# The bias of 30 experts copied into PSUM by ScalarE instead of multiplied in by TensorE

## The reference, cut to what matters

```python
def moe_ffn(h, w_router, b_router, w_gate_up, b_gate_up, w_down, b_down):
    logits = (xt @ w_router + b_router).astype(jnp.float32)
    top_val, top_idx = lax.top_k(logits, TOP_K)          # 4 of 32
    gates = jax.nn.softmax(top_val, axis=-1)
    ...
    def expert_block(args):                              # 128 tokens of one expert
        xb, e = args
        gu = xb @ w_gate_up[e] + b_gate_up[e]            # (128,1024) x (1024,2048)
        gate = jnp.minimum(gu[:, :D_FF], SWIGLU_LIMIT)
        up = jnp.clip(gu[:, D_FF:], -SWIGLU_LIMIT, SWIGLU_LIMIT)
        glu = gate * jax.nn.sigmoid(SWIGLU_ALPHA * gate)
        return ((up + 1.0) * glu) @ w_down[e] + b_down[e]
    ys = ys * slot_g[:, None]                            # each row by its gate
    out = jax.ops.segment_sum(ys, slot_tok, num_segments=T)
```

## Time and profile before

| | |
|---|---|
| time before, median of 3 (range) | 1756.38 us (1755.71 to 1757.04) |
| profiled execution: its time, its span | 1755.91 us, 1754.3 us |
| TensorE busy | 1731.1 us (99%) |
| VectorE busy | 1339.7 us (76%); 940.07 of the 1000 us from 700 to 1700 |
| ScalarE busy | 1120.1 us (64%) |
| GpSimd busy | 293.3 us (17%) |
| HBM traffic | 476.22 MB read, 28.36 MB written |

### The profile page before, as it was taken

One profiled execution on the slowest core, in us unless ns is written; L12 is line 12 of the kernel. 1 busy time (PEld: TensorE's weight loads), 2 busy tenths in 40 slices (PEclk: granted clock), 3 DMA queues, 4 the chain that ended last, 5 costly groups with the idle time before them and its releaser, 6 DMA issues.

```text
span 1754.3 us, 23536 instructions
## 1 busy us (share of the span) xinstructions
PE 1731.1 (99%) x8315; PEld 1410.9 (80%) x8316; DVE 1339.7 (76%) x1169; ACT 1120.1 (64%) x957; POOL 293.3 (17%) x228
## 2 busy tenths in 40 slices
PE   9999999999999999999999999999999999999996
PEld 7777888888887777888888888888888888888885
DVE  6323324343346898999999999999999999999998
ACT  5534334473222467777777777777777777777777
POOL 3000000000001262222222121212121212121211
PEclk9999999999999999999999999999999999999998
DMA  8322231212332599999999999999999999999995
GB/s 293 95 96 72 75 93 51 70 57 88 101 139 85 214 348 397 357 384 385 402 367 372 368 385 373 369 377 384 370 373 380 385 369 367 381 388 369 371 367 210
DMA packets 115728, 487.96 MB, mean 278 GB/s; under 512 B 18931, under 2 KB 49683, under 8 KB 66528
## 3 DMA queue, kind: packets, MB, share of 16 engines
q1 hardware_dynamic: 99576, 455.76, 67.9%
q0 software_dynamic: 16096, 31.54, 6.4%
q10 hardware_dynamic: 8, 0.01, 0.0%
HBM read 476.22 MB, written 28.36 MB: 288 GB/s over the span
## 4 chain that ended last, share of the span: by engine, by line
PE 94%; DVE 3%; ACT 2%; issue 1%; POOLq 0%; POOL 0%; DVEq 0%; ACTq 0%
PE psA L1717 22%; PE psA L1718 22%; PE psA L1719 22%; PE psX L1719 6%; PE psX L1718 6%; PE psX L1717 6%; PE psX L1724 3%; DVE wlo L1464 1%; PE psX L1911 1%; PE psX L1896 1%; PE psA L2128 1%; ACT whi L1003 1%; PE psX L1920 1%; PE psA L2008 0%; PE psX L1856 0%
## 5 line engine op out<-in xcount | busy, mean ns | idle before, releaser
L1464 DVE TENSOR_TENSOR wlo<-raw,whi 128x2048 fp32r<-128x2048 f32 x382 | 863.6, 2289 | 61.2 <-ACT whi L1003 60.2
L1003 ACT CAST whi<-raw 128x2048 fp32r<-128x2048 f32 x382 | 724.8, 1913 | 197.3 <-PE psA L1719 178.5
L1717 PE MATMUL psA<-whi,xT_hi 128*128 128x512 f32 x1036 | 408.3, 394 | 1.9 <-issue 1.9
L1719 PE MATMUL psA<-whi,xT_lo 128*128 128x512 f32 x1036 | 404.0, 390 | 0.0
L1718 PE MATMUL psA<-wlo,xT_hi 128*128 128x512 f32 x1036 | 403.9, 390 | 0.0
L1717 PEld LDWEIGHTS psA<-whi,xT_hi 128*128 128x128 f32 x1036 | 195.0, 188 | 43.1 <-issue 3.9
L1719 PEld LDWEIGHTS psA<-whi,xT_lo 128*128 128x128 f32 x1036 | 194.8, 188 | 40.7
L1718 PEld LDWEIGHTS psA<-wlo,xT_hi 128*128 128x128 f32 x1036 | 195.1, 188 | 39.6 <-issue 0.5
L1717 PE MATMUL psX<-whi,aT_hi 128*128 128x512 f32 x496 | 195.8, 395 | 0.0
L1719 PE MATMUL psX<-whi,aT_lo 128*128 128x512 f32 x496 | 193.5, 390 | 0.0
L1718 PE MATMUL psX<-wlo,aT_hi 128*128 128x512 f32 x496 | 193.3, 390 | 0.0
(11 more groups left out here) (408 smaller groups left out, 2025.2 us busy)
## 6 DMA issues: line engine op xcount, KB each, us to landing
raw<-in_w_gate_up SPq DMA_DIRECT2D x254, 1024.0 KB, 8.7
raw<-in_w_down SPq DMA_DIRECT2D x128, 1024.0 KB, 8.1
raw<-in_w_in SPq DMA_DIRECT2D x32, 1024.0 KB, 5.5
raw<-in_w_gla_proj SPq DMA_DIRECT2D x4, 1024.0 KB, 5.1
raw<-in_w_fox_proj SPq DMA_DIRECT2D x4, 1024.0 KB, 5.3
raw<-in_w_out SPq DMA_DIRECT2D x4, 1024.0 KB, 5.0
xt<-in_x SPq DMA_DIRECT2D x4, 512.0 KB, 7.3
h_dram<-xt POOLq DMA_DIRECT2D x4, 512.0 KB, 6.0
```

What stands on the lines that cost most here:

```text
L1003: s_.copy(xsplit(c)[0], xraw(slot)).then_inc(hi_ready, 1)
L1464: v.tensor_tensor(lo, xraw(slot), hi.bitcast(F32), ALU.subtract).then_inc(lo_ready, 1)
L1717: mm(dst, sh, mh, start=first, stop=False)
L1719: return mm(dst, sl, mh, start=False, stop=last)
```

## The change

From expert 2 on the bias no longer goes through TensorE.

- GpSimd loads the bias row of expert e (four pieces of 512 floats on partitions 0, 32, 64, 96) into `bias_row` and copies each over all 128 partitions with `partition_broadcast` into `bias_all` (128x4x512). The spread for expert i+2 stands in body i behind the gather and ahead of the scatter.
- ScalarE copies `bias_all` into `psA` (`seed(i+1)`, after expert i's silu) once VectorE has read the banks (`up_ev`) and the broadcasts are done (`bias_spread`); TensorE's first matmul of the next `gate_up` waits for `seeded`, and all of its matmuls add to what is there.
- `gate_up_bias` is gone for experts 2 to 31. Experts 0 and 1 and overflow blocks keep it.
- VectorE clips before its last subtraction of the body, waiting for the last gate-up tile (`tile_used`), and makes `act_t` before the first subtraction of the next expert. Its three copies are gone.
- GpSimd copies `gidx` and `didx` itself; ScalarE takes the gate column straight from `ltab`.
- Several one-shot semaphores are merged, and `lnffn_g` lies at another address.

```diff
+        def gather_index(i):
+            pool.wait_ge(index_ready, 2 * i - 3)
+            pool.wait_ge(xg_in, 16 * (i + 1))
+            g.tensor_copy(gidx[:], lrows[:, bass.ds(i + 2, 1)]).then_inc(index_ready, 1)
+        def scatter_index(i):
+            pool.wait_ge(y_out, 16 * (i - 1))
+            g.tensor_copy(didx[:], lrows[:, bass.ds(i - 1, 1)]).then_inc(index_ready, 1)
...
+        def load_row(e):
+            pool.wait_ge(bias_spread, 4 * (e - 2))
+            g.dma_start(bias_row[0:P:32, :], a["b_gate_up"][0][e].rearrange("(n c) -> n c", c=512)).then_inc(brow_in, 16)
+        def spread_row(e):
+            pool.wait_ge(brow_in, 16 * (e - 1))
+            pool.wait_ge(xg_in, 16 * e)
+            if isinstance(e, int) and e == 2:
+                pool.wait_ge(gu_done, 2)
+            else:
+                if not isinstance(e, int) or e > 3:
+                    pool.wait_ge(y_out, 16 * (e - 3))
+                pool.wait_ge(seeded, e - 2)
+            for n in range(4):
+                g.partition_broadcast(bias_all[:, n, :], bias_row[32 * n:32 * n + 1, :]).then_inc(bias_spread, 1)
+            pool.wait_ge(bias_spread, 4 * (e - 1))
...
         pool.wait_ge(routed, 1)
-        pool.wait_ge(gu_done, 2)
+        g.dma_start(bias_row[0:P:32, :], a["b_gate_up"][0][2].rearrange("(n c) -> n c", c=512)).then_inc(brow_in, 16)
+        spread_row(2)
         g.dma_start(lnffn_g[:], bcast(a["ln_ffn_g"][0])).then_inc(lnffn_in, 16)
...
         def body(i, last):
             if not last:
-                pool.wait_ge(gu_done, i + 1)
-                load_bgu(i + 1)
                 if not isinstance(i, int) or i < E - 2:
-                    gather(i + 3, i + 2)
+                    load_row(i + 2)
+                    if isinstance(i, int) and i == 1:
+                        gather(4, 3)
+                    else:
+                        gather_index(i)
+                        gather(None, i + 2)
             if isinstance(i, int) and 3 <= i < 3 + TT:
                 add_bias(i - 3, i)
+            if not last and (not isinstance(i, int) or i < E - 2):
+                spread_row(i + 2)
+            if not last and (not isinstance(i, int) or 2 <= i < E - 2):
+                scatter_index(i)
             scatter(i - 1)
...
+        def seed(e):
+            act.wait_ge(up_ev, e)
+            act.wait_ge(bias_spread, 4 * (e - 1))
+            s_.copy(psA[:], bias_all[:]).then_inc(seeded, 1)
...
             silu(i)
+            seed(i + 1)
             for c in range(XSPL):
                 step_hi(i + 1, c)
-            y_evac(i - 1, i + 3)
+            y_evac(i - 1)
...
-            if not first:
-                dve.wait_ge(y_out, 16 * (i - 1))
-                chain.mark(v.tensor_copy(didx[:], lrows[:, bass.ds(i - 1, 1)]))
-                chain.mark(v.tensor_copy(queue[:, 0, 1:2], ltab[:, bass.ds(i - 1, 1), 1]))
-                dve.wait_ge(xg_in, 16 * (i + 1))
-                chain.join()
-                v.tensor_copy(gidx[:], lrows[:, bass.ds(i + 2, 1)]).then_inc(tab_ready, 1)
...
-            for c in range(XSPL + 5, STEPC):
+            for c in range(XSPL + 5, STEPC - 1):
                 step_lo(i, c)
             swiglu_in(i)
+            step_lo(i, STEPC - 1)
             turned_lo(xT_hi_s, i + 2, xT_hi, xT_lo, xT_lo_s)
-            step_lo(i + 1, 0)
             swiglu_out(i)
-            for c in range(1, XSPL):
+            for c in range(XSPL):
                 step_lo(i + 1, c)
...
+        def gate_up_seeded(n, c):
+            tile_ready(n)
+            hi, lo = xsplit(c)
+            for b in range(4):
+                cols = slice(b * 512, (b + 1) * 512)
+                mm(psA[:, b, :], xT_hi[:, c, :], hi[:, cols], start=False, stop=False, skip_group_check=True)
...
-                pe.wait_ge(up_ev, i)
+                pe.wait_ge(seeded, i - 1)
...
-            gate_up_bias(i)
+            if first:
+                gate_up_bias(i)
```

More of the change, by code:

```diff
@@ L205, in build @@
     tokens = at("tokens", 104.5, [P, P])
-    lnffn_g = at("lnffn_g", 120, [P, D])
+    lnffn_g = at("lnffn_g", 203, [P, D])
     lnffn_b = at("lnffn_b", 172, [P, D])
@@ L756, in _ @@
                 e = pool.value_load(ovtab[0:1, bass.ds(j, 1)], min_val=0, max_val=E - 1)
-                gather(E + 4 + j, E + j)
+                gather(6 + j, E + j)
                 load_bgu(e)
@@ L1065, in y_evac_over, with y_evac @@
                           scale=queue[:, 0, 1:2]).then_inc(y_ready, 1)
-        def y_evac(i, free, src=psD):
+        def y_evac(i):
             act.wait_ge(tile_used, down_used(i))
-            act.wait_ge(tab_ready, free)
-            s_.activation(y_t[:], src.rearrange("p b c -> p (b c)"), ACT.Copy,
-                          scale=queue[:, 0, 1:2]).then_inc(y_ready, 1)
+            if isinstance(i, int) and i == 0:
+                act.wait_ge(tab_ready, 4)
+                gate = queue[:, 0, 1:2]
+            else:
+                act.wait_ge(y_out, 16 * i)
+                gate = ltab[:, bass.ds(i, 1), 1]
+            s_.activation(y_t[:], psD.rearrange("p b c -> p (b c)"), ACT.Copy, scale=gate).then_inc(y_ready, 1)
         act.wait_ge(xt_done, 1)
@@ L1092, in _ @@
         silu(1)
+        seed(2)
         for c in range(XSPL):
             step_hi(2, c)
-        y_evac(0, 4)
+        y_evac(0)
         turned_hi(aturn_done, 2, aT_hi, aT_hi_s)
@@ L1538, in swiglu_in, with swiglu_in_over, clip @@
         def swiglu_in(i):
-            dve.wait_ge(gu_done, i + 1)
+            if isinstance(i, int) and i < 2:
+                dve.wait_ge(gu_done, i + 1)
+            else:
+                dve.wait_ge(tile_used, gu_used(i))
+            clip(i)
+        def swiglu_in_over(j):
+            dve.wait_ge(gu_done, 3 + j)
+            clip(E + j)
+        def clip(i):
             v.tensor_scalar(by_pair(gate_t), psA[:, 0:2, :].rearrange("t b (q p k) -> t (b q) k p", p=P, k=2), LIMIT,
@@ L1620, in _ @@
         dve.wait_ge(ltab_in, 32)
-        seq.link(v.tensor_copy(lrows[:], ltab[:, :, 0]))
-        start = seq.used
+        v.tensor_copy(lrows[:], ltab[:, :, 0]).then_inc(index_ready, 1)
         with dve.Fori(2, E - 1) as i:
-            chain = Steps(dve, dve_seq, start + DVE_LOOP_LINKS * (i - 2))
-            body(i, chain)
-            body_used = chain.used
-        assert body_used == DVE_LOOP_LINKS, body_used
-        seq.used = start + body_used * (E - 3)
+            body(i, None)
         v.tensor_scalar(tokens[:], ident[:], ltab[:, E - 1, 0:1], None, ALU.mult).then_inc(match_seq, 1)
@@ L2095, in tile_ready @@
             pe.wait_ge(lo_ready, NCD + n + 1)
+        def gate_up_seeded(n, c):
[4 more added lines that the diff above has]
+                mm(psA[:, b, :], xT_hi[:, c, :], hi[:, cols], start=False, stop=False, skip_group_check=True)
+                mm(psA[:, b, :], xT_hi[:, c, :], lo[:, cols], start=False, stop=False, skip_group_check=True)
+                ins = mm(psA[:, b, :], xT_lo[:, c, :], hi[:, cols], start=False, stop=c == KT - 1,
+                         skip_group_check=True)
+            ins.then_inc(tile_used, 1)
         def gate_up(n, c, parts, after_first=False):
@@ L2186, in body @@
             else:
-                pe.wait_ge(up_ev, i)
+                pe.wait_ge(seeded, i - 1)
             for c in range(GUC):
-                gate_up(tile_no(i, c), c, (xT1_hi, xT1_lo) if first else (xT_hi, xT_lo), first and c == 0)
+                if first:
+                    gate_up(tile_no(i, c), c, (xT1_hi, xT1_lo), c == 0)
+                else:
+                    gate_up_seeded(tile_no(i, c), c)
                 if first:
@@ L2230, in _ @@
         split_ready(xT_hi_s, xT_lo_s, E)
-        pe.wait_ge(up_ev, E - 1)
+        pe.wait_ge(seeded, E - 2)
         for c in range(GUC):
-            gate_up(tile_no(E - 1, c), c, (xT_hi, xT_lo))
+            gate_up_seeded(tile_no(E - 1, c), c)
             if c == 2:
```

84 lines of the change are left out of this document (46 added, 38 removed).

## The result

| | before | after |
|---|---|---|
| median of 10 runs side by side (range) | 1756.17 us (1754.84 to 1758.90) | 1760.99 us (1757.48 to 1763.98) |
| ratio, 95% interval | | 1.0025 (1.0017 to 1.0033) |
| span of the profiled execution | 1754.3 us | 1760.2 us |

A forecast was written before the change was run, and what follows sets the result against it. TensorE, busy 94% of the span, bounds the kernel, VectorE 1.94 us behind. Bias -15.9, blocking +7.8 and first seed +15.4 sum to +7.3 on 1755.91: 1763.2, stated as 1763 us; range 1746 to 1780.

The forecast's parts named there:

- Bias off TensorE, -15.9: At the seam between matmuls and transposes on TensorE: the bias costs 0.53 us an expert, lost by 30 experts.
- L2128-like row: Sign of a right forecast: TensorE's profile shows no more such bias rows after expert 1.
- VectorE's copies: In VectorE's loop: removing them saves 0.51 us, leaving 32.58 us of own work an expert; slack only, no gain by itself.
- Broadcasts block VectorE, 2.19 us, +7.8: In the loop: three blocking broadcasts at 0.63 us and two copies at 0.15 make VectorE the bound at 34.77 us.
- the one witness: Earlier trace at 39 us: a subtraction behind a GpSimd operation took 3.12 us instead of 2.29; GpSimd's next 3.03, not 1.09.
- Rival 2: In the loop: broadcasts do not block, reading one partition and letting go early; TensorE bounds, 1755.4 us; chance 0.15.
- The first seed, +15.4: At expert 2, once: an uncovered wait, TensorE standing 13.7 us, plus 1.7 us for the lowered clock.
- Reload 8.1: Before expert 2's broadcasts: GpSimd's library reload takes 8.1 us, the middle of 6.0 to 10.3; floor 0.24.
- Bias row 6.0: At expert 2: the bias row, issued at 664.72, lands 6.0 us later, at 670.7.
- Broadcasts 2.5: At expert 2, after the reload: four broadcasts take 2.5 us, ending at 681.3, ahead of the seed.
- The rest: Broadcasts ahead of the scatter, one bias load for two, merged semaphores and moved `lnffn_g`: no cost.
- The seed covered in every body, by 2 us: In each loop body: seed, cast and subtraction finish at about 10.5 us; TensorE wants that tile at 12.5.

The follow-up runs named there:

- the best kernel: The changed kernel with a small broadcast at 568 us, an iota at 1735 us, and expert 2's bias back on TensorE: 1740.89 us, ratio 0.9913.

## Why the prediction came out as it did

The time was right, 1763 against 1761.0, and slower was the likeliest side. That it came so near is luck: two of its terms were wrong and one was missing, and the errors cancelled.

- *Bias off TensorE, -15.9.* Right. 0.57 us an expert in the periods, 17.0 us in the run without bias. The seam shows the forecast's 0.24 us (transposes start 0.23 us behind the last matmul), and no L2128-like row follows expert 1.
- *VectorE's copies.* Right: VectorE's own work was put at 32.58 us and is 32.5.
- *Broadcasts block VectorE, 2.19 us, +7.8.* Wrong. The step that failed took the one witness, where each side waited for the other's whole instruction, and charged 0.63 us for each of three broadcasts, besides 0.15 for each of two copies. Measured: 0.85 us for the four broadcasts, nothing that shows for the copies, period 34.46, nothing given back. GpSimd paid instead: four broadcasts take 8 to 9 us beside subtractions and 2.80 us alone, its copy of the gather's row numbers 2.85 us and not 0.15. Rival 2 was right on the loop, not on its reason; the point where VectorE becomes the bound does exist, and twice the broadcasts are beyond it. The Trainium skill (SBUF — State Buffer, Who interferes with whom) calls the ports that the two engines share an exclusive lock, and says of VectorE's two-port modes that the side that issues later is fully blocked for the other's whole instruction. Read so for these subtractions, GpSimd's records agree, VectorE's do not, since the longest subtraction of the run, 2.75 us, is 0.47 longer than one alone, against 0.70 for a broadcast.
- *The first seed, +15.4.* The size was near (17.4 us of idle time, and 1.7 by the clock), its parts were not. Reload 8.1: it took 5.90. The Trainium skill's approximately 6 us (GPSIMD Engine Reference, Instruction dispatch) agrees. Bias row 6.0: it landed in 3.56. Broadcasts 2.5: 2.81. What was missed is the start of the chain: the row was issued at 675.11 and not 664.72, 4.0 us of that by the start, 6.4 by list writes of 5.2 us. An execution without long writes does not have that last part. The gap of 17.4 us lay outside the 10 to 16 forecast.
- *"The rest" at nothing.* Wrong by 4.0 us. The prediction read the 0.24 us of the earlier trace rows as "the library was probably there already" and used that for the price of a reload, without asking who had left it there, and whether the changed kernel still would. It leaves the broadcast's library behind.
- *The seed covered in every body, by 2 us.* Right: the first subtraction behind the seed starts at 1107.71 and is over by 1110.0, and TensorE's `gate_up` begins at 1111.94. It holds only by the new order, which the old order's +92 us shows.

In the profiled executions expert 2 starts 20.4 us late and the end comes 5.9 us late, so all behind it gives 14.5 us: 30 x 0.57 = 17.1 less the clock's 1.7 is 15.4, and 0.9 us are not placed. In the runs: -17.0 for the bias, +12.4 for the two loadings, +7.7 for the rest of expert 2's seed, and the last 2.1 between the best kernel and the one without bias: +5.2. These four are differences of neighbouring medians and add up by construction; that the sum is not the 4.8 measured side by side is the kernel before's median, 1755.79 us in one set and 1756.17 in the other.

## What to carry to other kernels

A change that wins in the steady loop is decided at its first iteration and at the two ends of the launch: follow the first use of each new operation back to its inputs, and ask what state the launch leaves for the next. Where an engine's code must be swapped, put a dummy instruction where that engine waits anyway, one before the first use and one at the end that brings the start's code back; here two instructions turned 0.25% slower into 0.4% faster, and leaving the first iteration as it was made it 0.9%. And test a bundle's parts in both settings: the reordering was worth nothing alone and 92 us beside the seeds.

## What the runs showed of the hardware

- The code that GpSimd holds outlives a launch. With the broadcast last, the next launch stood 10.65 us before its first select; with an iota last, TensorE's first transposes started at 10.43 us in place of 13.98. Swapping the broadcast's code in took 5.90 and 6.04 us, and 6.95 where it began beside weight loads. In front of the iota that brings the start's code back GpSimd stood for 8.19 us.
- An indirect DMA's issue on GpSimd takes 0.98 us, or 5.23 where it starts 0.11 to 0.15 us behind a pair of VectorE's back-to-back subtractions out of two SBUF tiles, and 2.2 to 2.7 where it starts 0.4 to 0.9 us behind it, in all twelve profiles. The Trainium skill (SBUF — State Buffer, Who interferes with whom) explains a DMA that VectorE stalls by GpSimd starved of port time, and the rows fit that. Its remark that a `tensor_tensor` does not do it they contradict, since these subtractions are that instruction.
- The blocking of VectorE by GpSimd grew faster than the number of broadcasts: 0.85 us an expert for four, 1.5 more for another four. Why was not tried. A small copy on GpSimd beside subtractions took 2.85 to 4.64 us and cost VectorE nothing that shows.
- Behind the same 1.9 us of idle time on TensorE the granted clock fell in eight of the twelve profiled executions (0.57 to 0.67 in a stretch of 4 us) and stayed at 1.00 in four. A single profile of each kernel does not tell which of the two a kernel usually has.
